# Final norm and turning to rows moved from a stage of their own into the last pair of the second feed-forward

## The reference, cut to what matters

```python
def rmsnorm(x, g):
    x32 = x.astype(jnp.float32)
    y = x32 * lax.rsqrt(jnp.mean(x32 * x32, axis=-1, keepdims=True) + RMS_EPS)
    return (y * g.astype(jnp.float32)).astype(x.dtype)

def swiglu_ffn(x, g, w_gate, w_up, w_down):
    h = rmsnorm(x, g)
    return (jax.nn.silu(h @ w_gate) * (h @ w_up)) @ w_down
...
x <- x + 1/2 * SwiGLU_2(RMSNorm(x))
y = RMSNorm_final(x)
```

## Time and profile before

| | us |
|---|---|
| median of 3 runs | 2957.78 (2956.92 to 2965.39) |
| the profiled execution's own time | 2962.66 |
| its span, first to last instruction | 2960.8 |
| PE busy | 2700.4 (91%) |
| DVE busy | 1482.2 (50%) |
| ACT busy | 889.9 (30%) |
| POOL busy | 378.9 (13%) |

### The profile page before, as it was taken

The page is one execution under the profiler, slowest core; times in us unless marked ns, Lnnn a source line. Parts: engine busy times, 40 slices in busy tenths (PEclk is TensorE's granted clock), DMA queues, the critical chain, the costliest instruction groups (busy, mean ns, idle before and its releaser), DMA issues. The chain is left out here.

```text
span 2960.8 us, 45703 instructions
## 1 busy us (share of the span) xinstructions
PE 2700.4 (91%) x17724; PEld 2532.6 (86%) x17724; DVE 1482.2 (50%) x2848; ACT 889.9 (30%) x1563; POOL 378.9 (13%) x425
## 2 busy tenths in 40 slices
PE   4899988999999999999878888677999999999997
PEld 4898987999999999888866666447899999999996
DVE  4444446444444444454157677454364444554445
ACT  4656555111111111233256666332321111111102
POOL 3444430000000000000012222550000000000000
PEclk9999999999999999999979989898999999999999
DMA  4131315111111110031211010784212111111001
GB/s 175 61 122 62 122 63 156 50 43 43 43 43 43 43 43 28 19 115 44 87 59 40 26 44 33 249 262 147 58 45 56 43 43 43 43 56 57 28 0 59
DMA packets 166261, 206.47 MB, mean 70 GB/s; under 512 B 11342, under 2 KB 147407, under 8 KB 163370
## 3 DMA queue, kind: packets, MB, share of 16 engines
q1 hardware_dynamic: 154834, 142.29, 15.6%
q0 software_dynamic: 11296, 62.45, 5.9%
HBM read 190.87 MB, written 18.01 MB: 71 GB/s over the span
## 5 line engine op out<-in xcount | busy, mean ns | idle before, releaser
L406 ACT ACTIVATE f_act_gate<-f_act_gate 128x352 f32<-128x352 f32 x132 | 65.8, 498 | 1186.2 <-DVE f_act_gate L463 1186.2
L500 DVE SCALAR_TENSOR_TENSOR trunk<-f_down,trunk 128x352 f32<-128x352 f32 x528 | 276.0, 524 | 207.6 <-PE f_down L104 207.6
L102 PE MATMUL f_up<-f_h_hi,f_gu_hi 128*128 128x352 f32 x1056 | 344.5, 326 | 0.0
L102 PE MATMUL f_gate<-f_h_hi,f_gu_hi 128*128 128x352 f32 x1056 | 344.3, 326 | 0.0
L104 PE MATMUL f_up<-f_h_hi,f_gu_lo 128*128 128x352 f32 x1056 | 342.7, 325 | 0.0
L104 PE MATMUL f_gate<-f_h_hi,f_gu_lo 128*128 128x352 f32 x1056 | 342.5, 324 | 0.0
L102 PE MATMUL f_down<-f_a_hi,f_wd_hi 128*128 128x352 f32 x1056 | 340.6, 323 | 0.0
L103 PE MATMUL f_gate<-f_h_lo,f_gu_hi 128*128 128x352 f32 x1056 | 340.5, 322 | 0.0
L103 PE MATMUL f_up<-f_h_lo,f_gu_hi 128*128 128x352 f32 x1056 | 340.1, 322 | 0.0
L103 PE MATMUL f_down<-f_a_lo,f_wd_hi 128*128 128x352 f32 x1056 | 338.5, 321 | 0.0
L104 PE MATMUL f_down<-f_a_hi,f_wd_lo 128*128 128x352 f32 x1056 | 338.0, 320 | 0.0
(11 more groups left out here) (359 smaller groups left out, 5443.4 us busy)
## 6 DMA issues: line engine op xcount, KB each, us to landing
f_gu_raw<-in_w_ffn_gate_dram SPq DMA_DIRECT2D x44, 512.0 KB, 4.1
f_gu_raw<-in_w_ffn_up_dram SPq DMA_DIRECT2D x44, 512.0 KB, 5.4
f_wd_raw<-in_w_ffn_down_dram SPq DMA_DIRECT2D x22, 1024.0 KB, 5.0
as_pages<-in_cache_kv_slc_dram SPq DMA_DIRECT2D x128, 128.0 KB, 3.3
as_pages<-in_cache_kv_slc_dram POOLq DMA_DIRECT2D x128, 128.0 KB, 3.4
at_spread<-saved_rows SPq DMA_DIRECT2D x16, 768.0 KB, 4.1
x_saved<-trunk SPq DMA_DIRECT2D x2, 2112.0 KB, 13.7
trunk<-x_saved SPq DMA_DIRECT2D x3, 1408.0 KB, 7.7
```

Of the source, the lines that this page charges most:

```text
L102: pe.matmul(out, w_hi, x_hi, start=first, stop=False)
L406: act.activation(act_gate[:, b, :], act_gate[:, b, :], ACT.Silu).then_inc(silu_done, 1)
L500: dve.scalar_tensor_tensor(xT[:, m, chunk(c)], down_bank[n % 4][:, 0:CH], 0.5, xT[:, m, chunk(c)], ALU.mult, ALU.add).then_inc(down_free, 1)
```

## The change

`stage_finish` and `Norm` are gone. `stage_ffn` takes an argument `finish`, which f2 alone gets. In the last pair of f2:

- PE turns token tiles 0 to 4 of `trunk` itself, not yet normed, between down products (`TURNED_BEHIND`: tile 0 behind product (1, 1), that is chunk 1, feature tile 1; and so on), into a pair of banks of 1024 columns each, and tiles 5 to 8 behind the last product. Tiles 0 to 6 take the gate and up banks in turn, tiles 7 and 8 the down banks.
- ACT squares a turned tile out of PSUM and sums it along the row (`accum_out`), takes the root of a [tokens, 1] column, and scales the right half of the row out of PSUM by the inverse root.
- DVE adds epsilon, inverts with one Newton step on [tokens, 1] columns, and writes the left half, scaled by inverse root and gain; for tiles 5 and 8 it writes the whole row. Where these stand between the additions is set by `SQUARED_BEHIND` and `NORMED_BEHIND`.
- POOL multiplies the right half by the gain.
- SP loads the gain as a row spread over all partitions (512 KB) ahead of the last pair's weights, and stores each tile. The rows to be stored lie in the weight buffers `gu_raw` and `wd_raw`, six in all.
- PE's loop now ends a pair earlier, with the last pair written out, in f1 too. The eight banks are allocated as four tensors of two banks each.

The deleted class `Norm` and `stage_finish` are printed above and left out here, as is the new input (the gain as one row).

```diff
...
+class FinishRows:
+    def __init__(self, mem, scope, K, xT, gain_row, y_prompt, y_sample, pairs_of_banks, rows):
+        self.K, self.xT, self.gain_row, self.targets = K, xT, gain_row, (y_prompt, y_sample)
+        self.banks, self.y = pairs_of_banks, rows
+        self.gain = mem.sb(scope, "fin_gain", [P, D_MODEL])
+        self.junk = mem.sb(scope, "fin_junk", [P, D_MODEL])
+        self.sums, self.var, self.inv, self.tmp = [mem.sb(scope, "fin_" + name, [P, TT])
+                                                   for name in ("sums", "var", "inv", "tmp")]
+        self.gain_in, self.turned = mem.sem("fin_gain_in"), mem.sem("fin_turned")
+        self.summed, self.var_done, self.root_done = (mem.sem("fin_summed"), mem.sem("fin_var_done"),
+                                                      mem.sem("fin_root_done"))
+        self.inv_ready, self.scaled = mem.sem("fin_inv_ready"), mem.sem("fin_scaled")
+        self.left_done, self.right_done = mem.sem("fin_left_done"), mem.sem("fin_right_done")
+        self.out_sem = [mem.sem(f"fin_out{i}") for i in range(len(self.y))]
+        self.step = Order(mem.sem("fin_dve_step"))
+    def rows_of(self, t):
+        return P if t < TT - 1 else N_SAMPLE
+    def shared(self, t):
+        return t not in (5, TT - 1)
+    def rights(self, t):
+        return sum(self.shared(v) for v in range(t))
+    def load(self, sp):
+        sp.dma_start(self.gain[:], self.gain_row.to_broadcast([P, D_MODEL])).then_inc(self.gain_in, 16)
+    def store(self, sp):
+        for t in range(TT):
+            n = self.rows_of(t)
+            sp.wait_ge(self.left_done, t + 1)
+            if self.shared(t):
+                sp.wait_ge(self.right_done, self.rights(t) + 1)
+            target = self.targets[0][t * P:t * P + n, :] if t < TT - 1 else self.targets[1]
+            sp.dma_start(target, self.y[t % len(self.y)][0:n, :]).then_inc(self.out_sem[t % len(self.y)], 16)
+    def wait_stored(self, sp):
+        for i, sem in enumerate(self.out_sem):
+            sp.wait_ge(sem, 16 * len(range(i, TT, len(self.y))))
+    def wait_room(self, engine, t):
+        if t >= len(self.y):
+            engine.wait_ge(self.out_sem[t % len(self.y)], 16 * (t // len(self.y)))
+    def turn(self, pe, t):
+        n, bank = self.rows_of(t), self.banks[t]
+        for k in range(KT):
+            tr = pe.transpose(bank[0:n, k * P:(k + 1) * P], self.xT[:, k, t * P:t * P + n], self.K["ident"][:])
+        tr.then_inc(self.turned, 1)
+    def wait_taken(self, pe, t):
+        pe.wait_ge(self.left_done, t + 1)
+        if self.shared(t):
+            pe.wait_ge(self.scaled, self.rights(t) + 1)
+    def square(self, act, t):
+        n = self.rows_of(t)
+        act.wait_ge(self.turned, t + 1)
+        if t:
+            act.wait_ge(self.summed, t)
+        act.activation(self.junk[0:n, :], self.banks[t][0:n, :], ACT.Square, scale=D_MODEL ** -0.5,
+                       accum_out=self.sums[0:n, t:t + 1]).then_inc(self.summed, 1)
+    def root(self, act, t):
+        n = self.rows_of(t)
+        act.wait_ge(self.var_done, t + 1)
+        act.activation(self.inv[0:n, t:t + 1], self.var[0:n, t:t + 1], ACT.Sqrt).then_inc(self.root_done, 1)
+    def scale_right(self, act, t):
+        n, y = self.rows_of(t), self.y[t % len(self.y)]
+        act.wait_ge(self.inv_ready, t + 1)
+        self.wait_room(act, t)
+        act.activation(y[0:n, BANK:D_MODEL], self.banks[t][0:n, BANK:D_MODEL], ACT.Copy,
+                       scale=self.inv[0:n, t:t + 1]).then_inc(self.scaled, 1)
+    def gain_right(self, pool, t):
+        n, y = self.rows_of(t), self.y[t % len(self.y)]
+        pool.wait_ge(self.scaled, self.rights(t) + 1)
+        pool.tensor_tensor(y[0:n, BANK:D_MODEL], y[0:n, BANK:D_MODEL], self.gain[0:n, BANK:D_MODEL],
+                           ALU.mult).then_inc(self.right_done, 1)
+    def mean_square(self, dve, t):
+        n = self.rows_of(t)
+        dve.wait_ge(self.summed, t + 1)
+        dve.tensor_scalar(self.var[0:n, t:t + 1], self.sums[0:n, t:t + 1], EPS, None, ALU.add).then_inc(self.var_done, 1)
+    def invert_and_left(self, dve, t):
+        n, y, step = self.rows_of(t), self.y[t % len(self.y)], self.step
+        var, inv, tmp = [x[0:n, t:t + 1] for x in (self.var, self.inv, self.tmp)]
+        dve.wait_ge(self.var_done, t + 1)
+        dve.wait_ge(self.root_done, t + 1)
+        step.did(dve.reciprocal(inv, inv))
+        step.wait(dve)
+        step.did(dve.scalar_tensor_tensor(tmp, inv, inv, var, ALU.mult, ALU.mult))
+        step.wait(dve)
+        step.did(dve.tensor_scalar(tmp, tmp, -0.5, 1.5, ALU.mult, ALU.add))
+        step.wait(dve)
+        dve.tensor_tensor(inv, inv, tmp, ALU.mult).then_inc(self.inv_ready, 1)
+        dve.wait_ge(self.inv_ready, t + 1)
+        self.wait_room(dve, t)
+        width = BANK if self.shared(t) else D_MODEL
+        dve.scalar_tensor_tensor(y[0:n, 0:width], self.banks[t][0:n, 0:width], inv, self.gain[0:n, 0:width],
+                                 ALU.mult, ALU.mult).then_inc(self.left_done, 1)
+def stage_ffn(nc, mem, K, xT, gain, w_gate, w_up, w_down, name, copies=(), copied=None,
+              finish=None):
@@ -343,9 +323,10 @@
         a_hi = mem.sb(scope, name + "_a_hi", [P, 2, T], F32R)
         a_lo = mem.sb(scope, name + "_a_lo", [P, 2, T], F32R)
         act_gate = mem.sb(scope, name + "_act_gate", [P, 2, CH])
-        gate_bank = [mem.ps(scope, f"{name}_gate{i}") for i in range(2)]
-        up_bank = [mem.ps(scope, f"{name}_up{i}") for i in range(2)]
-        down_bank = [mem.ps(scope, f"{name}_down{i}") for i in range(4)]
+        gate_banks, up_banks = mem.ps(scope, name + "_gate", (P, 2 * BANK)), mem.ps(scope, name + "_up", (P, 2 * BANK))
+        down_banks = [mem.ps(scope, f"{name}_down{i}", (P, 2 * BANK)) for i in range(2)]
+        gate_bank, up_bank = [[x[:, i * BANK:(i + 1) * BANK] for i in range(2)] for x in (gate_banks, up_banks)]
+        down_bank = [x[:, i * BANK:(i + 1) * BANK] for x in down_banks for i in range(2)]
         sum_bank = down_bank[0]
         gu_landed = [mem.sem(f"{name}_gu_landed{s}") for s in range(2)]
@@ -361,6 +342,16 @@
         ONE = 1
         UNITS = 2 * CHUNKS
         DOWNS = KT * CHUNKS
+        if finish:
+            gain_row, y_prompt, y_sample, others_stored = finish
+            rows = [x[:].rearrange("p s k n -> p s (k n)")[:, i, :] for x in gu_raw for i in range(2)]
+            rows += [wd_raw[:, i, :] for i in range(2)]
+            order = [(gate_banks, up_banks)[t % 2] for t in range(7)] + down_banks
+            fin = FinishRows(mem, scope, K, xT, gain_row, y_prompt, y_sample, order, rows)
+            TURNED_BEHIND = {(1, 1): 0, (1, 4): 1, (2, 1): 2, (2, 3): 3, (2, 5): 4}
+            SQUARED_BEHIND = {(1, 3): 0, (1, 6): 1, (2, 3): 2, (2, 5): 3, (2, 7): 4}
+            NORMED_BEHIND = {(1, 4): 0, (1, 7): 1, (2, 4): 2, (2, 6): 3}
         with nc.Block() as block:
             @block.gpsimd
@@ -369,6 +360,11 @@
                     pool.wait_ge(gu_split[1], 1 + ONE)
                 for target, source in copies:
                     pool.dma_start(target, source).then_inc(copied, 16)
+                if finish:
+                    pool.wait_ge(fin.gain_in, 16)
+                    for t in range(TT):
+                        if fin.shared(t):
+                            fin.gain_right(pool, t)
             @block.sync
             def _(sp):
@@ -388,7 +384,14 @@
                 load_gu(0, 0, 0)
                 with sp.Fori(0, PAIRS - 1) as i:
                     pair(i, False)
+                if finish:
+                    fin.load(sp)
                 pair(PAIRS - 1, True)
+                if finish:
+                    fin.store(sp)
+                    for sem, count in others_stored:
+                        sp.wait_ge(sem, count)
+                    fin.wait_stored(sp)
             @block.scalar
             def _(act):
@@ -433,6 +436,23 @@
                 with act.Fori(1, PAIRS - 1) as i:
                     pair(i, False)
                 pair(PAIRS - 1, True)
+                if finish:
+                    for s in range(2):
+                        act.wait_ge(gu_split[s], PAIRS + ONE)
+                    act.wait_ge(wd_split, PAIRS + ONE)
+                    for t in range(6):
+                        fin.square(act, t)
+                        fin.root(act, t)
+                        if fin.shared(t):
+                            fin.scale_right(act, t)
+                    fin.square(act, 6)
+                    fin.square(act, 7)
+                    fin.root(act, 6)
+                    fin.scale_right(act, 6)
+                    fin.square(act, 8)
+                    fin.root(act, 7)
+                    fin.scale_right(act, 7)
+                    fin.root(act, 8)
             @block.vector
             def _(dve):
@@ -473,6 +493,12 @@
                     dve.wait_ge(dve_step, u + 1)
```

(57 more changed lines are left out.)

166 lines of the change are left out of this document (2 added, 164 removed).

## The result

| | before | after |
|---|---|---|
| median of the runs (lowest to highest), us | 2958.36 (2956.92 to 2965.39), 5 runs | 2933.04 (2931.99 to 2942.53), 5 runs |
| after over before | | 0.9916, 95% interval 0.9904 to 0.9929 |
| profiled execution, its span | 2962.66, 2960.8 | 2937.25, 2935.4 |
| third addition of the last pair begins | 2891.51 | 2890.89 |
| last addition ends, us behind that | 20.55 | 27.33 |

The kernel is 25.3 us (0.8%) faster by the medians, where 22.5 were forecast: 2933.0 against 2935.3. The executions of the changed kernel are spread over 10.5 us, so medians alone can't say that a forecast was met to 2 us; the profile has to.

The account below looks back on a forecast made before the run. PE bounds up to the last addition, then a 48.7 us chain over ACT, PE and DVE; -48.7 + 7.1 + 19.1 = -22.5 us takes 2962.66 to 2940.2, and the median, 4.9 lower, to 2935.3 (range 2931 to 2944).

Parts of the forecast that it names:

- What bounds: PE bounds up to the last addition at 2912.06; then 48.7 us of last stage, an ACT, PE and DVE chain.
- The down products: Last pair's products: last addition +7.1 us, from five turns (4.4), 1.5 of waiting and 1.2 of DVE's work.
- The wait in front of turn 4: Inside the down products: PE waits 1.5 us for both halves of tile 2, whose inverse follows addition (2,4).
- The table load: Inside the down products: ACT's 1.28 us load of the root's table, between square 0 and root 0, is covered.
- Behind the last addition: From the last addition's end at 2919.2 to the span's end at 2938.3: 19.1 us.
- I take 2.0 us for a turn: Behind the last addition: PE's clock falls to half after idling, so turns of tiles 6 and 7 take 2.0 us.
- signs of being wrong: Whole last pair: PE gaps, clock 0.5 between 2899 and 2917, last addition behind 2922, column steps over 0.25 us, POOL-held store.
- The 0.03 for a hand-over between engines: Throughout the new chain: a hand-over costs 0.03 us, read from the table load's end to the next activation.
- A: Rival: PE's clock falls inside the down products, +13.4 us, so 2949; chance 0.08.
- B: Rival: small steps dearer or early tiles not overlapped, 2943.5 with none hidden; with D, 2938 to 2944, chance 0.24.
- C: Rival: fetching 1728 written-out PE instructions stalls; win gone at 13 ns each, 2970 at 20 ns; chance 0.03.
- D: Rival: last tiles still gate everything, only barrier and wide steps are won; B's far end, together 0.24.

Follow-up runs that it names:

- e5: Changed kernel with the transposes of tiles 0 to 3 done twice; 49.12 us from the third addition to the span's end, against 44.51.
- e3: Changed kernel with DVE's epsilon and inverse of tile 2 one addition earlier; 44.26 us from the third addition to the span's end, against 44.51.
- e2: Changed kernel with all nine tiles turned, squared and scaled behind the last down product; 2943.08 us, ratio to before 0.9955.
- e9: Changed kernel profiled once more, unchanged; 45.18 us from the third addition to the span's end, 17.81 of it behind the last addition.
- e1: Kernel before, with only PE's last pair written out in both feed-forwards; 2956.92 us, ratio to before 1.0001.
- e8: e3 with other banks, so PE turns tiles 5, 6 and 7 at once behind the last addition; 43.19 us from third addition to end.
- e6: Changed kernel with DVE alone scaling whole rows, no ACT right halves or POOL gains; 46.47 us from third addition to end, against 44.51.

## Why the prediction was right

**What bounds.** Right: from f2's table load to the third addition nothing changed (728.0 us, as before), and all that was won lies behind it.

**The down products,** +7.1 forecast, +6.78 measured. The five turns were 0.87 each, and e5 shows that they add their own length and no more. The wait in front of turn 4 came where I put it, for the reason given, the inverse of tile 2 behind addition (2,4): 1.20 us on PE, 1.46 on the loads, against 1.5. e3 took it away and moved the last addition by 1.37. What is left, 6.78 - 4.35 - 1.37 = 1.06, is DVE's own work in front of the last addition, 1.2 in the forecast. The table load was covered, as e2 shows from the other side.

**Behind the last addition,** 19.1 forecast, 17.18 measured; this term was mis-sized by 1.9. It splits at the end of square 7. Up to there I had 8.3 us (2927.5 - 2919.2), and measured are 6.2: the accumulator of square 7 is read at 2924.42, and the last addition ended at 2918.22. The step that failed is "I take 2.0 us for a turn": turns 6 and 7 took 0.87 each, at full clock. In e3, where the clock fell, the same stretch took 7.51: so 1.3 of the 2.1 us are the clock, and 0.8 were priced too high even for half clock. Two turns and a hand-over had 4.2 us there, and in e3 square 7 begins 3.72 us behind the first load of turn 6 (2913.70 - 2909.98); the square with its sum had 1.25 and took 1.11. That the clock stayed full was luck in part: the same kernel lost it for one turn in e9, and 17.81 lies nearer to the 19.1. From square 7 to the last row's end I had 7.6, and 7.64 were measured, out of two errors that cancel. The root was 0.20 and not 0.28, and the square with its sum 1.1 and not 1.25, since the read overlaps it. Against that stood the 0.5 us of the held L285, which I had not foreseen: I had priced the step at 0.21 from a row in which POOL was idle. The last 3.34 us are the 3.2 of the forecast. So one of the signs of being wrong did come, a column step over 0.25 us, but once and for 0.5 us. The 0.03 for a hand-over between engines was read from two rows of one engine, ACT, 0.02 apart; between engines after has 0.03 from DVE's epsilon to ACT's root (2918.92 to 2918.95) and 0.11 from the root back to DVE (2919.15 to 2919.26), which the shorter root covers.

**The sum.** -22.5 forecast, -24.8 in the profile, -25.3 by the medians.

**The rivals.** A, the clock falling inside the products, did not come: 1.00 up to 2924. B, dearer small steps and no overlap, did not come: the steps were cheaper except for the hold, and the overlap is worth about 9. Its price for no overlap was sound, 14 us won, where e2 won 15.2. C is refuted by e1. D would have left e2's 54.05, and it was 44.51.

**The rule that I weighed.** The turns among products and the 24 transposes behind 2920.93 ran at a granted clock of 1.00, while e2, whose turns were 3 us apart, stood at 0.50 and rose to 0.96 when three turns followed on each other, with no matmul of another kind for 20 us. So here full clock was kept, and came back, on transposes alone. What decides near the edge isn't shown: after and e9 are the same kernel and differ. The Trainium skill, "TensorE: Matmul & The Clock Gate", Part 4: PE-mode transpose, says that full clock doesn't engage for them; the measurements differ from it, and they decide.

## What to carry to other kernels

Where a stage behind the last matmul is a chain of small steps over several engines, cut the data into tiles along the axis that the last loop finishes first, and start the chain inside that loop. Most of what is won (15.2 of 24.8 us here) can come from the shorter chain itself, so build that alone first to know which part pays. Let PE's turns follow on each other instead of one by one, where the banks allow it: the profiles speak for it (e2 against e8), though none isolates it. Keep column steps that run beside POOL to one SBUF tensor.

## What was not expected of the hardware

- **DVE held by POOL.** L285 over 32x1 took 0.21 us with POOL idle (e6) and 0.71 while POOL multiplied two SBUF operands, and it ended with POOL's instruction; with one tensor and two column pointers it took 0.26 beside POOL. An addition with one input in PSUM was not held (0.53 us at 2904.09, while POOL ran from 2903.41 to 2904.71). The Trainium skill, "SBUF — State Buffer", Who interferes with whom, says that a DVE instruction with two SBUF inputs and a GpSimd one that reads SBUF exclude each other for the whole instruction; the trace agrees for DVE's side, with 0.71 against 0.21; POOL's instructions took 1.26 to 1.30 us throughout, so none is seen waiting for DVE.
- **The clock near its edge.** The same kernel ended its last three turns at full clock in one profile (1.74 us for 16 loads) and at half for one turn in another (1.57 for 8, then 2.31 for 16), for 0.63 us of the end. Before and e1 differ by 0.94 us in the old last stage, and in its clock too.
- **Written-out code.** 1728 more instructions in PE's code, in place of the loops' last turns, gave 1.0001 times the time, interval 0.9991 to 1.0011.
- **A stage that repeats to 0.1 us behind one that doesn't.** Ahead of f2's table load, kernels that are the same up to there stood up to 11 us apart (2153.46 to 2164.51); from it to the third addition they took 728.0 us each. What makes the first part vary was not tried.
